# Where the second half of the modulation is multiplied: behind the score products instead of behind the input projections

## The reference, cut to what matters

```python
mod = jax.nn.silu(c) @ w_ada[l] + b_ada[l]                  # (2 groups, 6 * 1024)
sh1, sc1, g1, sh2, sc2, g2 = jnp.split(mod[:, None, :], 6, axis=-1)
h = rms_norm(x, norm_mix[l]) * (1.0 + sc1) + sh1
m, s_hg, s_gla = token_mixer(h, ...)                         # 4 HGRN2 heads, 4 GLA heads, chunked recurrence
x = x + g1 * m
h = rms_norm(x, norm_ffn[l]) * (1.0 + sc2) + sh2
x = x + g2 * hierarchical_moe(h, ...)                        # 32 experts, two per token
```

## Time and profile before

| what | value |
|---|---|
| time, median of 3 runs | 1661.51 us (1658.68 to 1661.53) |
| the profiled execution | 1659.88 us, its span 1658.0 us |
| TensorE busy | 93% of the span, 12836 products |
| VectorE, ScalarE, GpSimd busy | 72%, 56%, 18% |
| granted TensorE clock, mean | 0.974 |
| mixers: units 2 to 5 | from 373.18 us to about 764 us of the span |

### The profile page before, as it was taken

How to read it: one execution, slowest core, us unless ns; L and a number is a source line. 1 busy time by engine, 2 the same in 40 slices (tenths; PEclk the granted TensorE clock), 3 DMA queues, 4 the chain that set the end, 5 groups by cost and what they waited for, 6 DMA issues and landing times. The chain is left out here.

```text
span 1658.0 us, 30197 instructions
## 1 busy us (share of the span) xinstructions
PE 1541.9 (93%) x12836; PEld 1352.8 (82%) x12836; DVE 1197.3 (72%) x1537; ACT 921.3 (56%) x1094; POOL 301.5 (18%) x203
## 2 busy tenths in 40 slices
PE   5999999999999999997998985999999999999956
PEld 4899999999889989896996863888888888888842
DVE  5753682468476675758565467999999999999947
ACT  5542454337353463633112214888888888888832
POOL 1320020001010010102000001132354342232130
PEclk9999999999999999998999996999999999999978
DMA  9221023111324162323446338999999999999965
GB/s 330 54 78 40 16 69 105 29 41 59 103 78 148 59 189 90 96 97 135 156 163 221 128 138 306 349 369 387 381 382 391 389 385 389 385 384 396 370 234 231
DMA packets 129663, 346.12 MB, mean 209 GB/s; under 512 B 16464, under 2 KB 72504, under 8 KB 103864
## 3 DMA queue, kind: packets, MB, share of 16 engines
q1 hardware_dynamic: 113704, 312.29, 52.1%
q0 software_dynamic: 9824, 17.88, 2.9%
q10 hardware_dynamic: 6000, 13.99, 2.3%
HBM read 316.04 MB, written 43.81 MB: 217 GB/s over the span
## 5 line engine op out<-in xcount | busy, mean ns | idle before, releaser
L149 PE MATMUL wo_psum_m<-h_hi,x_w_hi 128*128 128x364 f32 (+1 forms) x1184 | 403.3, 341 | 9.5 <-DVE h_lo L1475 3.3
L150 PE MATMUL wo_psum_m<-h_lo,x_w_hi 128*128 128x364 f32 (+1 forms) x1184 | 389.7, 329 | 0.0
L151 PE MATMUL wo_psum_m<-h_hi,x_w_lo 128*128 128x364 f32 (+1 forms) x1184 | 389.5, 329 | 0.0
L149 PEld LDWEIGHTS wo_psum_m<-h_hi,x_w_hi 128*128 128x128 f32 x1184 | 223.1, 188 | 23.9 <-issue 10.0
L150 PEld LDWEIGHTS wo_psum_m<-h_lo,x_w_hi 128*128 128x128 f32 x1184 | 223.4, 189 | 2.5
L151 PEld LDWEIGHTS wo_psum_m<-h_hi,x_w_lo 128*128 128x128 f32 x1184 | 223.2, 189 | 0.0
L737 POOL CAST x_w_hi<-x_w 128x1024 fp32r<-128x1024 f32 x44 | 73.4, 1668 | 608.3 <-PE wo_psum_m L151 588.2
L2326 POOL DMA_INDIRECT scratch_y<-e_y,all_tbl x32 | 74.2, 2319 | 371.8 <-ACT e_y L2452 371.8
L1468 DVE TENSOR_TENSOR x_w_lo<-x_w,x_w_hi 128x1024 fp32r<-128x1024 f32 x52 | 64.3, 1236 | 93.0 <-POOL x_w_hi L737 61.6
L149 PE MATMUL e_psum_g<-e_g_hi,e_x_hi 128*128 128x512 f32 x256 | 105.0, 410 | 3.2 <-DVE e_x_lo L2559 2.6
L151 PE MATMUL e_psum_g<-e_g_hi,e_x_lo 128*128 128x512 f32 x256 | 101.7, 397 | 0.0
(11 more groups left out here) (388 smaller groups left out, 3520.0 us busy)
## 6 DMA issues: line engine op xcount, KB each, us to landing
mg_ring_hi<-in_w_e_gate SPq DMA_DIRECT2D x34, 1024.0 KB, 10.4
mg_ring_lo<-in_w_e_down SPq DMA_DIRECT2D x34, 1024.0 KB, 9.2
mg_ring_hi<-in_w_e_up SPq DMA_DIRECT2D x32, 1024.0 KB, 9.1
mg_ring_lo<-in_w_e_up SPq DMA_DIRECT2D x32, 1024.0 KB, 9.3
mg_ring_lo<-in_w_e_gate SPq DMA_DIRECT2D x30, 1024.0 KB, 10.7
mg_ring_hi<-in_w_e_down SPq DMA_DIRECT2D x30, 1024.0 KB, 9.3
x_w<-in_w_in SPq DMA_DIRECT2D x44, 512.0 KB, 4.0
scratch_gate<-x_x ACTq DMA_DIRECT2D x16, 544.0 KB, 3.5
```

What stands on the lines that cost most here:

```text
L149: nc.tensor.matmul(out, lhs[0], rhs[0], start=start, stop=False)
L150: nc.tensor.matmul(out, lhs[0], rhs[1], start=False, stop=False)
L151: return nc.tensor.matmul(out, lhs[1], rhs[0], start=False, stop=stop)
```

## The change

The 32 pieces move to 15 places behind score products in the loops of units 2 to 5. The place (u, -1) is behind `scores(u, 0)`, the place (u, j) behind the scores of pass j. Units 2, 3 and 4 have places -1, 0, 4 and 6 with two, one, three and three pieces; unit 5 has places -1, 0 and 2 with two, one and two. A chunk's four pieces no longer accumulate in one go: the pieces of one chunk at one place form a part, there are 19 parts, and VectorE adds each part to late_mod with four additions, in place of the one addition per chunk and row group (32 before, 76 after). SP issues a piece's load behind the weight load that its place follows. At SP's end, the loads of the mixed rows move ahead of the two gate rows and the store of late_mod, and the gate rows' semaphores become three.

```diff
-        LATE_FIRST, LATE_CHUNKS = 2 * D // 512, {3: (0, 3), 4: (3, 6), 5: (6, 8)}
...
+        LATE_FIRST, LATE_PIECES = 2 * D // 512, 32
+        late_points = {(u, j): n for u in (2, 3, 4) for j, n in ((-1, 2), (0, 1), (4, 3), (6, 3))}
+        late_points.update({(5, -1): 2, (5, 0): 1, (5, 2): 2})
...
+        def late_load(p):
+            u, j = late_point[p]
+            done = [(u, middle(u)[-1])] + [block for j_ in range(j) for block, c in filled(u, j_)]
+            return load_no[done[-1]] + 1
...
+            def late_piece(p):
+                if p == 0:
+                    sp.wait_ge(o_out[1], out_landed(NU, 1))
+                    sp.wait_ge(proj_done, place[(1, "logit"), NC - 1] + 1)
+                if p >= 3:
+                    sp.wait_ge(late_done, p - 2)
+                c0, k0 = (LATE_FIRST + p // 4) * 512, 2 * (p % 4)
+                sp.dma_start(late[p % 3][:, :, :], w_ada[:, k0:k0 + 2, c0:c0 + 512]).then_inc(late_in[p % 3], 16)
...
-                for p in [p for c in range(NC) for p in late_at.get((*loads[n - 1], c), ())] if n else ():
...
+                for p in range(LATE_PIECES):
+                    if late_load(p) == n:
+                        late_piece(p)
...
+            def late_ada(u, j):
+                for no, (point, _, pieces) in enumerate(late_parts):
+                    if point != (u, j):
+                        continue
+                    at = (1 + no % 3) * P
+                    pe.wait_ge(state_ready, u * (NT + 1) + max(j, 0))
+                    before = sum(1 for at_, _, _ in late_parts if at_ < point)
+                    if before:
+                        pe.wait_ge(late_kept, before)
+                    for p in pieces:
+                        pe.wait_ge(late_in[p % 3], 16 * (p // 3 + 1))
+                        for i in range(2):
+                            for r in range(4):
+                                m = nc.tensor.matmul(p_u[32 * r:32 * r + 2, at:at + P], c_cols[:, 2 * (p % 4) + i, :], ...)
+                        m.then_inc(late_done, 1)
...
                 if sub == SUB[u] - 1:
+                    if (u, j) in late_points:
+                        pe.wait_ge(late_kept, sum(1 for point, _, _ in late_parts if point <= (u, j)))
                     nc.tensor.matmul(p_u[:, 0:SUB[u] * DV], tok[0:n, i % 2, 0, :],
...
                         project(u, name, c)
-                        late_ada(u, name, c)
...
                 scores(u, 0)
+                late_ada(u, -1)
...
                             scores(u, j + ahead_)
+                    late_ada(u, j)
                     for (of, name), c in filled(u, j):
...
-                if u in LATE_CHUNKS:
-                    keep_late(u)
                 mask(u, 0)
                 for j in range(NS[u]):
                     if j + 1 < NS[u]:
                         mask(u, j + 1)
+                    if j == 0:
+                        keep_late(u, -1)
+                    keep_late(u, j)
                     advance(u, j)
```

More of the change, by code:

```diff
@@ L610, in mixers @@
             s.sem("last_exp"), s.sem("last_scaled"), s.sem("last_ready"), s.sem("last_hi"), s.sem("last_lo"))
-        gate_in = [s.sem(f"gate_in{i}") for i in range(2)]
+        gate_in = [s.sem(f"gate_in{i}") for i in range(3)]
         a_done, b_done_m, a_gated, b_gated, piece_done = (
@@ L625, in mixers @@
         mod_rows = mod_d.rearrange("g (j r c) -> g j r c", r=4, c=P)
-        LATE_FIRST, LATE_CHUNKS = 2 * D // 512, {3: (0, 3), 4: (3, 6), 5: (6, 8)}
[L627 to L631, removed]
+        LATE_FIRST, LATE_PIECES = 2 * D // 512, 32
+        late_points = {(u, j): n for u in (2, 3, 4) for j, n in ((-1, 2), (0, 1), (4, 3), (6, 3))}
+        late_points.update({(5, -1): 2, (5, 0): 1, (5, 2): 2})
+        late_parts, late_point = {}, []
+        for point, n in late_points.items():
+            first_ = len(late_point)
+            late_point += [point] * n
+            for p in range(first_, first_ + n):
+                late_parts.setdefault((point, p // 4), []).append(p)
+        late_parts = [(point, j, pieces) for (point, j), pieces in late_parts.items()]
+        def late_load(p):
+            u, j = late_point[p]
+            done = [(u, middle(u)[-1])] + [block for j_ in range(j) for block, c in filled(u, j_)]
+            return load_no[done[-1]] + 1
         w_cols = a["w_in"].rearrange("l (k p) c -> p (l k) c", p=P)
@@ L691, in gate_rows @@
                 for half in range(2):
-                    sp.dma_start(gates[i][half][:, :], gate_d[i + half * KD]).then_inc(gate_in[i % 2], 16)
+                    sp.dma_start(gates[i][half][:, :], gate_d[i + half * KD]).then_inc(gate_in[i % 3], 16)
             branch_weights(0)
             branch_weights(1)
[L696 to L702, removed]
+            for p in range(LATE_PIECES):
+                if late_load(p) == len(loads):
+                    late_piece(p)
             sp.wait_ge(proj_done, len(order))
@@ L706, in _ @@
                 sp.dma_start(land[:, row, :], mix_d[row]).then_inc(land_in[n // NB], 16)
+            sp.wait_ge(gate_out[0], 16 * (G0[NU] // 2))
+            sp.wait_ge(gate_out[1], 16 * (G0[NU] // 2 - 1))
+            sp.wait_ge(late_done, LATE_PIECES)
+            gate_rows(0)
+            sp.wait_ge(late_kept, len(late_parts))
+            for r in range(4):
+                sp.dma_start(mod_rows[:, LATE_FIRST:, r, :], late_mod[32 * r:32 * r + 2]).then_inc(late_out, 16)
             branch_weights(2)
@@ L784, in project @@
                 m.then_inc(proj_done, 1)
[L786 to L798, removed]
+            def late_ada(u, j):
[10 more added lines that the diff above has]
+                        for i in range(2):
+                            for r in range(4):
+                                m = nc.tensor.matmul(p_u[32 * r:32 * r + 2, at:at + P], c_cols[:, 2 * (p % 4) + i, :],
+                                                     late[p % 3][:, i, r * P:(r + 1) * P], start=(p == pieces[0] and i == 0),
+                                                     stop=(p == pieces[-1] and i == 1))
+                        m.then_inc(late_done, 1)
             def turn(u, i):
@@ L868, in last_square @@
                     pe.wait_ge(state_ready, NU * (NT + 1))
+                    pe.wait_ge(late_kept, len(late_parts))
                 if c == 2:
@@ L1514, in merged_low, with keep_late @@
                                 ALU.subtract).then_inc(m_lo_done, 1)
[L1516 to L1522, removed]
+            def keep_late(u, j_):
+                for no, (point, j, pieces) in enumerate(late_parts):
+                    if point != (u, j_):
+                        continue
+                    at = (1 + no % 3) * P
+                    if no == 0:
+                        dve.wait_ge(late_bias, 64)
+                    else:
+                        dve.wait_ge(late_kept, no)
+                    dve.wait_ge(late_done, sum(n for at_, n in late_points.items() if at_ <= point))
                     for r in range(4):
@@ L1525, in keep_late @@
                         m = V.tensor_tensor(late_mod[rr, j, :], p_u[rr, at:at + P], late_mod[rr, j, :], ALU.add)
-                m.then_inc(late_kept, 1)
+                    m.then_inc(late_kept, 1)
             cond.prepare(dve)
@@ L1636, in _ @@
             for i in range(KD):
-                dve.wait_ge(gate_in[i % 2], 32 * (i // 2 + 1))
+                dve.wait_ge(gate_in[i % 3], 32 * (i // 3 + 1))
                 for c in range(NC):
```

## The result

The changed kernel takes 1682.70 us (median of four runs, 1681.70 to 1684.21) against 1661.52 for the kernel before (1658.68 to 1661.81): 1.3% slower, ratio 1.0130 with a 95% interval of 1.0117 to 1.0143. The forecast was 1668.5 with a range of 1662.5 to 1674: the sign was right, the size was not, +21.2 us where +8 was worked out. The profiled execution took 1683.32 us, its span 1681.4, 23.4 longer than that of before.

What follows compares the result with a forecast made beforehand. TensorE bounds loops and second stretches, ScalarE's chain limits first-stretch gains. -16.06 middles, +8.50 first two places, +13.51 other pieces and places, +2.00 clock: +7.95 on 1659.88 gives 1667.8, set at 1668.5; range 1662.5 to 1674.

Steps and rivals of the forecast that it cites:

- The middles: Middles of units 3 to 5: removing pieces and places saves 6.86 us in second stretches, 9.20 in first; sum -16.06.
- ScalarE's copy of x0: First stretch, q to g0: its chain keeps 27.73 us; about 6 us removed becomes waiting. Rival without this hold: 1662.5, chance 0.08.
- The first two places: Unit 2, (2, -1) and (2, 0): TensorE waits for the second piece, landing at 440; +8.50 us, bounds 6.7 and 11.3.
- The low clock behind a long wait: Unit 2 after the hole of about nine us: work at the 1.2 GHz level costs 2.0 us, bounds 0 and 2.4.
- The wait of rows 13: Unit 5's end, TensorE waiting for VectorE before the last products: granted clock 0.50 to 0.54 over six us.
- The pieces and places: Loops: 32 pieces keep 0.43 us each, 13.76; 15 places at 0.08 add 1.20, bounds 0 and 4.8.
- the two readings of the Trainium skill: Pieces behind scores: same mode, a place costs nothing; width as mode, 0.32 us each. Rival places as switches: 1672.1, chance 0.06.
- My 0.08: Loops: assumed cost in us of each place behind score products, a quarter of the 0.32 switch.
- VectorE: Loops: 76 additions delay nothing because the filling projection covers the state product's wait; 0 us, bounds 0 and 0.4.
- 1.2 per part: Loops: cost in us per part that a place would have if the filling projection's cover were gone.

Runs made afterwards that it cites:

- additions early: Changed kernel with VectorE's additions of place (u, -1) put between mask(u, 0) and mask(u, 1): 1669.56 us, ratio 1.0059 to the kernel before.
- both: Changed kernel, additions of (u, -1) ahead of mask(u, 1), no unit 2 pieces before pass 4, two behind q in units 3 to 5: 1661.15 us, ratio 1.0000 to before.
- the two shifted kernels: 256 more already satisfied waits near the start of TensorE's program, added to the kernel before (1674.01 us) and to "both" (1670.42 us).
- spread: All 32 pieces laid out anew, also behind q and g0, none at (u, 0), additions of (u, -1) ahead of mask(u, 1): 1658.47 us, ratio 0.9979 to before.

## Why the prediction was right in sign and wrong in size

The middles: -16.06 worked out, -15.8 measured. That ScalarE's copy of x0 would hold the first stretch at 27.7 is shown twice over, by the wait of 1.59 us and by two pieces put back there at no cost.

The first two places: the second piece was put at 440 and came at 440.06, in an execution that ran 1.3 us later by then. That the number is met so closely is in part luck: the store landed in 2.8 us, faster than either bound, and the piece took 5.0, between the two. With the additions early, unit 2's loop is 14.1 longer than before; 8.50, 2.00 and 2.74 for the six other pieces make 13.2. With the first pieces moved away as well, in "both", 2.7 of the 14.1 are left, the price of those six. The low clock behind a long wait, for which the Trainium skill was named ("TensorE: Matmul & The Clock Gate", section HAM oscillation), came as that page has it, at 0.50. The wait of rows 13, from which the 2.0 was taken, stands before the first product of the branches (764.40), not before the mixers' last ones as I wrote; the clock behind it was read rightly.

The pieces and places: 0.43 a piece holds. A place costs nothing: in "both", the stretch from unit 3's scores to the filling projection is 4.55 us against 3.24, 1.31 for three pieces at two places, 1.29 at 0.43 each. Of the two readings of the Trainium skill, "TensorEngine Tiling (Array Packing)", sections Tiling Modes and Key Properties, the one by which score products and pieces share a mode is the one the runs agree with. My 0.08 was 1.2 us too much.

VectorE is the step that failed: "The cover is the filling projection that stands in every pass with a place. ... Nothing, bounds 0 and 0.4." I followed the additions to the state product alone, which waits behind the projection, and there the cover did hold. But the piece of (u, 0) waits for the additions of (u, -1) as well, in front of the projection, where there is no cover; these additions stand on VectorE behind mask(1), and this behind scores(1), which TensorE multiplies just ahead of that piece. The line that does it, `pe.wait_ge(late_kept, before)`, is in the diff, and no sentence of the prediction prices it, nor does a rival; its "1.2 per part" is for the state product, should the cover be gone. The rows for it were there: mask(1) ends at 535.28 + 0.29, four additions of 0.29 bring that to 536.8, and TensorE is at the place at 534.49, where the projection started; 2.3 us late in each of units 2 to 4, and 3.5 in unit 5 with its eight additions. Measured were 2.0 in unit 3 (1.57, and 0.40 lost inside the scores just ahead, which shortened the wait) and 3.7 in unit 5.

What this step cost: 8.7 us of waits, and behind two of them the half clock. The edit of three lines that takes all but 0.9 us of it away brought 13.1 us by the medians and 11.8 by the ratios (0.71% of 1661), and left 1669.56, one microsecond from the forecast by the median and 2.8 by the ratio. So most of the miss is this one wait with what hangs on it. The rest of the sum closes within 1 us in units 2 to 4, but not in unit 5, where 4.5 us were added to the loop in place of 2.4, 1.9 of it in the longer hole near its end. That the total comes so near the forecast is in part luck: in that trace middles and loops add 11.2 us where the sum had 7.95, and 2.9 come off behind the mixers, where it had nothing.

What stays open is how the place of packets in the stream and the traffic of other queues set the length of such holes; the two shifted kernels show that they move with the stream, not what a layout without them would cost.

## What to carry to other kernels

When a producer is made to wait for a reader's release of a shared bank, price the wait at every instruction that carries it, the first one above all, and look at what stands ahead of the release on the reader's engine. Where a wait is unavoidable, move the work it waits for into a gap that the reader already has: here one call, moved ahead of a mask on VectorE, was worth 12 to 13 us. Work moved off a stretch that another engine ends gives back only the part down to that engine; fill such a stretch first: up to the length of the wait that stands there it was free here (two pieces with their place, 1.18 us, in a wait of 1.59).

## What was not expected of the hardware

TensorE's instructions arrive in packets of 16 KB (103 packets, 1.69 MB on the page), some 125 products each. Passes of score products, some ten nanoseconds apart (48 in 0.46 us), seem to use them up faster than the next arrives: holes of 0.4 to 3.8 us that the profile labels issue, also in the middle of a run of like products, moved by 64 products when the stream was shifted by half a packet. That more small products right behind the scores make it worse was not shown: with at most two pieces there, "spread" still has holes of 0.60 and 2.82 us.

Holes of almost one length went with different clocks: 1.57 us at (3, 0) was followed by 1.00, 1.63 at (4, 0) by 0.50 for over three us of projections. No run here shows what decides it.
